# A two-block transformer kernel: the start in two channel halves, and four adaptive sums shared between VectorE, GpSimd and TensorE

## What is computed

```
c_act = silu(c)                                    # c: 1024 numbers
mod = c_act @ w_ada + b_ada                        # w_ada: 1024 x 6144
shift1, scale1, gate1, shift2, scale2, gate2 = split(mod, 6)
h = rms_norm(x, norm1_w) * (1 + scale1) + shift1
proj = h @ w_in                                    # gq, gk, gv, gz, ga, gb, sq, sk, sv
qkv = silu(causal_conv(concat(gq, gk, gv), conv_w, width 4))
...  gated delta rule on 8 heads, window attention on 8 heads
x = x + gate1 * (concat(o_g, o_s) @ w_out)
h2 = rms_norm(x, norm2_w) * (1 + scale2) + shift2
x = x + gate2 * ((silu(h2 @ w_gate) * (h2 @ w_up)) @ w_down)
```

## Time and profile before

| | |
|---|---|
| median of 3 runs | 1274.04 us (1273.92 to 1275.78) |
| profiled execution, its own time | 1273.12 us |
| its span in the profile | 1271.2 us |
| PE busy | 1221.3 us, 96% of the span |
| DVE, ACT, POOL busy | 701.7, 492.0, 107.0 us |
| chain that ended last | PE 91%, DVE 3%, DMA 2%, ACT 2% |

### The profile page before, as it was taken

How to read it: one execution, slowest core, us unless ns; L and a number is a source line. 1 busy time by engine, 2 the same in 40 slices (tenths; PEclk the granted TensorE clock), 3 DMA queues, 4 the chain that set the end, 5 groups by cost and what they waited for, 6 DMA issues and landing times.

```text
span 1271.2 us, 20461 instructions
## 1 busy us (share of the span) xinstructions
PE 1221.3 (96%) x8672; PEld 994.5 (78%) x8672; DVE 701.7 (55%) x1018; ACT 492.0 (39%) x774; POOL 107.0 (8%) x151
## 2 busy tenths in 40 slices
PE   2899999997999999999999999999999999999998
PEld 2577788787878888888888889798767678888886
DVE  4699878654468544323333457758456546334344
ACT  4543543665246323112222344223446663232232
POOL 4000004621011000000000110000012320000000
PEclk9899999999999999999999999999999999999999
DMA  9666621000222535233322343333231115433311
GB/s 311 219 209 184 219 66 36 3 3 31 74 67 71 163 105 160 81 111 104 100 87 63 86 146 94 100 92 76 41 79 46 34 47 134 115 87 87 114 40 67
DMA packets 150955, 125.62 MB, mean 99 GB/s; under 512 B 16985, under 2 KB 134514, under 8 KB 150737
## 3 DMA queue, kind: packets, MB, share of 16 engines
q1 hardware_dynamic: 147888, 119.88, 31.3%
q0 software_dynamic: 1232, 2.07, 0.5%
q10 hardware_dynamic: 1744, 2.36, 0.5%
HBM read 122.20 MB, written 2.10 MB: 98 GB/s over the span
## 4 chain that ended last, share of the span: by engine, by line
PE 91%; DVE 3%; DMA 2%; ACT 2%; issue 1%; POOL 0%; ACTq 0%; DVEq 0%; POOLq 0%
PE bank L583 56%; PE bank L676 5%; PE bank L825 5%; PE bank L1255 4%; PE bank L1226 4%; PE bank L1289 3%; PE bank L1143 2%; DMA arena<-in_meta_tokens_dram 1%; PE bank L988 1%; PE bank L1117 1%; PE bank L834 1%; PE bank L1176 1%; PE bank L1198 1%; PE bank L1156 1%; PE bank L797 1%
## 5 line engine op out<-in xcount | busy, mean ns | idle before, releaser
L583 PE MATMUL bank<-hsplit,whi 128*128 128x512 f32 (+1 forms) x1872 | 551.9, 379 | 0.7 <-DVE wlo L2005 0.7
L583 PEld LDWEIGHTS bank<-hsplit,whi 128*128 128x128 f32 x1872 | 341.2, 188 | 73.0 <-issue 8.0
L583 PE MATMUL bank<-hsplit,wlo 128*128 128x512 f32 (+1 forms) x936 | 352.3, 376 | 0.0
L2005 DVE TENSOR_TENSOR wlo<-ring,whi 128x2048 fp32r<-128x2048 f32 (+4 forms) x97 | 196.9, 2029 | 178.1 <-ACT whi L1485 177.8
L1485 ACT ACTIVATE whi<-ring 128x2048 fp32r<-128x2048 f32 (+4 forms) x97 | 165.4, 1705 | 129.3 <-DVE xT L2355 53.3
L583 PEld LDWEIGHTS bank<-hsplit,wlo 128*128 128x128 f32 x936 | 175.9, 188 | 33.1
L583 PE MATMUL bank<-a_split,whi 128*128 128x512 f32 x340 | 104.6, 389 | 0.0
L583 PEld LDWEIGHTS bank<-a_split,whi 128*128 128x128 f32 x340 | 63.8, 188 | 13.2
L583 PE MATMUL bank<-a_split,wlo 128*128 128x512 f32 x170 | 66.1, 389 | 0.0
L2034 DVE SCALAR_TENSOR_TENSOR post<-ring,small,post 128x512 f32<-128x512 f32 x77 | 57.9, 752 | 3.1 <-DMA ring<-in_w_ada_dram 0.4
L1426 POOL TENSOR_TENSOR acc<-acc,tb 128x512 f32<-128x512 f32 x12 | 17.7, 1478 | 426.2 <-ACT tb L1723 426.2
(11 more groups left out here) (443 smaller groups left out, 1726.2 us busy)
## 6 DMA issues: line engine op xcount, KB each, us to landing
ring<-in_w_ada_dram SPq DMA_DIRECT2D x24, 1024.0 KB, 5.2
ring<-in_w_in_dram SPq DMA_DIRECT2D x22, 1024.0 KB, 5.3
ring<-in_w_in_dram SPq DMA_DIRECT2D x34, 512.0 KB, 5.1
ring<-in_w_gate_dram SPq DMA_DIRECT2D x11, 1024.0 KB, 5.4
ring<-in_w_up_dram SPq DMA_DIRECT2D x11, 1024.0 KB, 5.2
ring<-in_w_down_dram SPq DMA_DIRECT2D x8, 768.0 KB, 4.9
ring<-in_w_down_dram SPq DMA_DIRECT2D x8, 640.0 KB, 4.5
ring<-in_w_out_dram SPq DMA_DIRECT2D x4, 1024.0 KB, 5.3
```

Source lines behind the costliest of these rows:

```text
L583: last = mm(o[0:m, 0:n], w[:, k, c0:c0 + m], rhs(s, k), start=k + i == 0, stop=k == kn - 1 and i == 2)
L2005: split_lo = splitter(dve, None, lambda lo, src, hi: tt(lo, src, hi, ALU.subtract))
```

## The change

- The ring loses `ada0` to `ada3`. They get places of their own, and SP issues x, `ada2`, `ada0`, `qkv0`, `ada3`, `ada1`, `qkv1`, `qkv2` without a wait. c comes as eight rows and is turned by PE.
- For i = 0 to 3 DVE sums only the first 512 rows. PE takes the second 512 straight from the panel: 16 matmuls of one column, and then the four of before.
- The modulation goes by channel halves: chunks 0 to 3 need columns i = 2 and 0, chunks 4 to 7 need i = 3 and 1. PE does `ada(3)` after chunk 1 and `ada(1)` after chunk 3 of the first tiles.
- DVE copies four chunks of x out of PSUM, ACT the other four.
- The meta tokens' columns come after the first tiles, their scaling after DVE's convolution of tile 1.
- For i = 4 to 7 DVE sums the first 512 rows; POOL makes four products and three additions for the second; PE adds both sums in PSUM, with eight matmuls in place of four. The slot of `ada{i}1` is free when POOL is done, and POOL starts panel i when PE has finished `ada(i - 1)`.
- POOL also clears `gates`, which DVE did before.

```
+        early_ada = {(i, h): hscratch[:, (2 * n + h) * PANEL:(2 * n + h + 1) * PANEL] for n, i in enumerate((2, 0)) for h in range(2)}
+        early_ada |= {half: C1.take(PANEL) for half in ((3, 0), (3, 1), (1, 0))}
...
+        POOL_ADA = range(4, 8)
+        pool_acc, pool_tmp = acc_buf[:, 0:512], row_buf
...
-        for i in range(4):
-            ada_panel(i)
...
+            def ada(i):
+                o = open_tile(pe, "ada", i)
+                if i < 4:
+                    pe.wait_ge(*ada_loaded(i, 1))
                     for k in range(4):
-                        last = mm(o[0:1, :], cs[:, 4 * h + k:4 * h + k + 1], W(f"ada{i}{h}")[:, k, :],
-                                  start=h + k == 0, stop=h == 1 and k == 3)
-                    last.then_inc(*(fill("adar", i) if h else signal("adarow_half", i)))
...
                 pe.wait_ge(*done("adaacc", i))
                 for c in range(4):
-                    last = mm(o[:, c:c + 1], adaacc[i % 2][:, c * P:(c + 1) * P], ones[:, 0:1], start=True, stop=True)
+                    last = mm(o[:, c:c + 1], acc_of(i)[:, c * P:(c + 1) * P], ones[:, 0:1], start=c == 0 if i in POOL_ADA else i >= 4,
+                              stop=i >= 8 or i < 4 and c == 3)
+                if i in POOL_ADA:
+                    pe.wait_ge(*done("poolacc", i))
+                    for c in range(4):
+                        last = mm(o[:, c:c + 1], pool_acc[:, c * P:(c + 1) * P], ones[:, 0:1], start=False, stop=c == 3)
...
+            tr(open_tile(pe, "c")[:, 0:KD], c_rows, ident[0:KD, 0:KD]).then_inc(*fill("c"))
+            pe.wait_ge(*arrived("x"))
...
-            ada(0)
+            pe.wait_ge(*copied("c"))
+            ada(2)
+            norm_spread("1", diag)
...
-            ada(1)
-            norm_spread("1", diag)
-            o = open_tile(pe, "spreadmeta")
-            pe.wait_ge(*done("dve_vectors", "diagmeta"))
-            mm(o[:, 0:META], ones[0:META, :], rbc[0:META, 0:META], start=True, stop=True).then_inc(*fill("spreadmeta"))
-            ada_rows(3)
-            ada(2)
-            ada_turn(3)
+            ada(0)
+            def meta_columns():
...
-                    first_tiles("qkv0", h_ready("1"), [(("pj", c), P * c, T, hx) for c in range(2)])
+                    first_tiles("qkv0", h_ready("1"), [(("pj", c), P * c, T, hx) for c in range(2)],
+                                between={1: [(ada, 3)], 3: [(ada, 1)]})
+                    meta_columns()
...
+            def load_ada(i):
+                for h in range(2):
+                    sp.dma_start(ada_half(i, h), w_cols(w_ada, 512 * i, 512, 4 * h, 4)).then_inc(sem(f"ld_ada{i}{h}"), 16)
+            sp.dma_start(x_in, a["x"][0].rearrange("(b p) f -> p b f", p=P)).then_inc(sem("ld_x"), 16)
+            load_ada(2)
+            load_ada(0)
             for i, (name, kn, width, parts) in enumerate(panels):
+                if name == "qkv1":
+                    load_ada(3)
+                    load_ada(1)
+                if name == "ada40":
+                    sp.dma_start(consts[:, CONST_FIRST:], a["consts"][:, CONST_FIRST:]).then_inc(sem("ld_const_rest"), 16)
...
+                    if before[:3] == "ada" and int(before[3:-1]) in POOL_ADA:
+                        sp.wait_ge(*done("poolacc" if before[-1] == "1" else "adaacc", int(before[3:-1])))
...
+            pool.wait_ge(*done("adaacc", 1))
+            nc.gpsimd.memset(gates, 0.0).then_inc(*signal("gates0"))
+            for i in POOL_ADA:
+                pool.wait_ge(*loaded(f"ada{i}1"))
+                if i > 4:
+                    pool.wait_ge(*filled("ada", i - 1))
+                w = W(f"ada{i}1")
+                for k in range(4):
+                    dst = pool_tmp[k % 2] if k else pool_acc
+                    nc.gpsimd.tensor_tensor(dst, w[:, k, :], cs[:, 4 + k:5 + k].broadcast_to([P, 512]), ALU.mult)\
+                        .then_inc(*signal("poolmul", i, k))
+                    if k:
+                        pool.wait_ge(*done("poolmul", i, k))
+                        nc.gpsimd.tensor_tensor(pool_acc, pool_acc, dst, ALU.add)\
+                            .then_inc(*(signal("poolacc", i) if k == 3 else signal("poolsum", i, k)))
+                        if k < 3:
+                            pool.wait_ge(*done("poolsum", i, k))
...
+            act.dma_start(c_rows, a["c"][0].rearrange("(k p) -> k p", p=P)).then_inc(sem("ld_c"), 16)
...
-            for k in range(KD):
+            for k in range(KD // 2, KD):
                 act.wait_ge(*filled("x", k))
                 A(xT[:, k, :], bank("x", k)[:, :], ACT.Copy).then_inc(*read("x", k))
...
+            def modulate_half(half):
+                act.wait_ge(*done("modA1", half))
+                act.wait_ge(*copied("ada", half))
+                first = 4 * half
+                for k in range(first, first + 5):
+                    if k < first + 4:
+                        act.wait_ge(*done("xn1", k))
+                        A(hpre[:, k, :], hpre[:, k, :], ACT.Identity, scale=modA1[:, k:k + 1],
+                          bias=modT[:, k:k + 1]).then_inc(*signal("mod1", k))
+                    if k > first:
+                        act.wait_ge(*done("mod1", k - 1))
+                        hi_part("h1", (k - 1,), h_of("1", 0, k - 1), hpre[:, k - 1, :])
...
+            modulate_half(0)
+            modulate_half(1)
...
+                halves = 1 if i < 8 else 2
...
+            for k in range(KD // 2):
+                dve.wait_ge(*filled("x", k))
+                v.tensor_copy(xT[:, k, :], bank("x", k)[:, :]).then_inc(*read("x", k))
+            dve.wait_ge(*copied("c"))
+            ada_sum(2)
+            spread("1", diag)
             ada_sum(0)
...
+            scale_half(0)
+            ada_mod(0)
+            split_lo()
+            h_rest("1", range(2))
+            ada_sum(3)
+            h_rest("1", range(2, 4))
             ada_sum(1)
...
+            scale_half(1)
+            ada_mod(1)
+            h_rest("1", range(4, 8))
...
+                if m == 1:
+                    meta_scaled()
```

More of the change, by code:

```diff
@@ L266, in program, with ada_half, ada_loaded @@
         gate_acc = C1b.take(2 * P)
+        early_ada[1, 1] = C1b.take(PANEL)
+        POOL_ADA = range(4, 8)
+        pool_acc, pool_tmp = acc_buf[:, 0:512], row_buf
+        def ada_half(i, h):
+            return early_ada[i, h].rearrange("p (k n) -> p k n", k=4) if i < 4 else W(f"ada{i}{h}")
+        def ada_loaded(i, h):
+            return arrived(f"ada{i}{h}") if i < 4 else loaded(f"ada{i}{h}")
         diag3 = arena[:, 10 * T:11 * T].rearrange("p (b t) -> p b t", b=4)
@@ L283, in program, with acc_of @@
         adaacc = [post[:, 0:512], post[:, 512:1024]]
+        def acc_of(i):
+            return adaacc[{2: 0, 0: 1, 3: 0}.get(i, i % 2)]
         G1, G2 = Cut(arena, base1), Cut(hscratch)
@@ L1464, in _ @@
                 act.wait_ge(*done("xss", b))
-            A(hpre[0:META, 0:2, :], meta_in[0:META, :].rearrange("p (k t) -> p k t", k=2), ACT.Square,
-              accum_out=msum[0:META, 0:1]).then_inc(*signal("act_vectors", "mss"))
             act.wait_ge(*done("dve_vectors", "eps"))
-            act.wait_ge(*done("act_vectors", "mss"))
             A(sroot, ssum, ACT.Sqrt, bias=epsc, scale=1.0 / D).then_inc(*signal("act_vectors", "root1"))
-            A(msum[0:META, 0:1], msum[0:META, 0:1], ACT.Sqrt, bias=epsc[0:META, :], scale=1.0 / D)\
-                .then_inc(*signal("act_vectors", "rootmeta"))
-            for k in range(KD):
+            for k in range(KD // 2, KD):
                 act.wait_ge(*filled("x", k))
                 A(xT[:, k, :], bank("x", k)[:, :], ACT.Copy).then_inc(*read("x", k))
-            act.wait_ge(*filled("meta"))
-            A(hmeta, bank("meta")[:, 0:8 * META], ACT.Copy).then_inc(*read("meta"))
             def root(tag, out, key, scale, bias):
@@ L1484, in _ @@
             A(V2[:, :], bank("vec")[:, P:P + V2_N], ACT.Copy).then_inc(*read("vec"))
+            act.wait_ge(*arrived("meta"))
+            A(tball[0:META, 0:D], meta_in[0:META, :], ACT.Square, accum_out=msum[0:META, 0:1]).then_inc(*signal("act_vectors", "mss"))
+            act.wait_ge(*done("act_vectors", "mss"))
+            A(msum[0:META, 0:1], msum[0:META, 0:1], ACT.Sqrt, bias=epsc[0:META, :], scale=1.0 / D)\
+                .then_inc(*signal("act_vectors", "rootmeta"))
             split_hi = splitter(act, lambda hi, src: A(hi, src, ACT.Copy), None)
@@ L1509, in _ @@
             split_hi()
-            act.wait_ge(*filled("adar", 3))
-            A(row_buf[1][0:1, :], bank("adar", 3)[0:1, :], ACT.Copy).then_inc(*read("adar", 3))
-            act.wait_ge(*done("dve_vectors", "modA1"))
-            modulate("1", modA1, 0)
+            modulate_half(0)
+            modulate_half(1)
             split_hi()
@@ L1535, in _ @@
                     conv_in(m)
+                    if m == 1:
+                        act.wait_ge(*filled("meta"))
```

(24 more changed lines are left out.)

93 lines of the change are left out of this document (36 added, 57 removed).

## The result

The change makes the kernel slower: 1289.72 us median of 6 runs (1287.69 to 1295.22) against 1274.01 for the kernel before, a ratio of 1.0129 [1.0108, 1.0149]. The profiled execution took 1288.9 us, with a span of 1287.0 against 1271.2: +15.8.

A forecast was written before the change was run, and what follows sets the result against it. PE, busy 96% of the span, was taken as the bound. Start -0.3, extra matmuls +3.9 and waits +5.9 gave +9.5 on 1273.12, so 1282.6, with the median 0.9 above: 1283.5 us, range 1274.5 to 1293.

The forecast's parts named there:

- Steps 1 to 4: Start: x loaded by 9.2 us, transposed by 14.3, `ada(2)` done at 20.3, `norm_spread` and the vectors at 22.7.
- step 3: Start, `ada(2)`: 20 matmuls mostly at the high clock, 15.1 to 20.3 us, with DVE's half sum about 3.1.
- Steps 5 to 8: From `ada(0)` (6.1 us) through first projection at 32.2, first tiles and meta columns: tile 2 at 62.1, start -0.3 us.
- My bound of +8: The start's upper bound: with the clock low throughout it gives +19 us, of which +8 was kept.
- Step 9: Tiles 2 to 11, PE: eight matmuls in place of four in `ada(4)` to `ada(7)`, 3.9 us, not hidden.
- Step 10: Tiles 2 to 11, DVE: saves 12.5 us of sums, worth nothing where PE never waited for them.
- Step 11: Tiles 2 to 11: POOL and DVE alternate, 11.7 us a panel on POOL; DVE loses 5.3 a panel, 21 in all.
- Step 12: After tile 4: a late panel split holds up ACT's squares, so PE waits 2.4 us.
- Step 13: `qkv5` queues behind `ada61`, whose slot waits for POOL: PE waits 2.3 us after tile 8, then 1.2 for `abk`.
- POOL and DVE don't hinder each other: Rival for the middle: start as forecast, then only PE's extra +3.9 us, 1277.6; chance 0.12.
- two rivals in which the start pays: Start -7.5 us: with no waits later 1270.4 (chance 0.10), or with the middle taking back 9.8, 1276.3 (0.12).
- low clock nearly throughout: Rival: `ada(2)` and `ada(0)` 8.6 us each, first projection near 39, tile 2 at 70, +8 + 9.8: 1292; chance 0.13.

The follow-up runs named there:

- `start_only`: The changed kernel's start with the middle of the kernel before, in which POOL sums nothing: 1278.93 us, ratio 1.0040 to the kernel before.
- `pool_narrow`: The changed kernel with POOL's products and additions over 32 of the 512 columns: 1281.85 us, ratio 1.0058 to the kernel before.
- `dve_pad`: `start_only` with seven more two-input DVE operations behind each of the sums for i = 4 to 7, and nothing on POOL: 1299.13 us.
- `pool_beside`: `start_only` with POOL also making 16 products and 12 additions from the constants, which no one uses or waits for in the tiles: 1299.48 us.
- `slot_free`: The changed kernel with POOL reading constants, and each second half's slot free once DVE has its half sum and the panel has landed: 1286.12 us.
- `middle_only`: The kernel before with POOL's part in the sums for i = 4 to 7 as in the changed kernel: 1287.65 us.

## Why the prediction was right, and where its sizes were off

The direction and the reason were right: 1283.5 was forecast, 1289.7 came, and a won start that PE pays back inside the first tiles, extra matmuls, and waits at `head_lengths` are all in the trace. The size was off: +15.7 for +9.5, inside the range but just outside the forecast's own band of 1278.5 to 1289. Most of the 6 us is a term of the clock, at the start and behind the wait. Point by point:

- **Steps 1 to 4** held: x at 10.1 (9.2), transposes to 15.98 (14.3), `ada(2)` to 20.4 (20.3), the vectors to 21.9 (22.7). DVE's half sum is 2.8 us by the earlier trace rows (0.5 and three of 0.78) and not the 3.1 of step 3; nothing waited for it.
- The page that the prediction weighed, the Trainium skill's "TensorE: Matmul & The Clock Gate", Part 4, by which transposes don't count as busy: the first `ada(2)`, straight behind the 32 transposes of x, ran at the high clock (3.70 us for 32 records, has 0.98 for 8), so this trace too speaks against it. In the nine profiles with this start those records took 3.70 to 4.84 us, and never the 6.84 of the low clock.
- **Steps 5 to 8**, the start at -0.3, were mis-sized: +4.3 in the profile and +5.9 by `start_only`. The term is the clock. `ada(0)` took 8.6 us and not 6.1, at 0.50 throughout, the first projection came at 33.6 and not 32.2, and chunks 2 and 3 took 4.8 and not 3.1, since `ada(3)` had let the clock fall. The two sums and the restart had nearly the right size (5.5, 5.8 and 3.1 for 5.2, 5.2 and 3.1). My bound of +8 held it.
- **Step 9**: 3.65 for 3.9, shown in the traces by blocks of 0.91 us and by `pool_narrow` (3.6 between the same two points); that fewer matmuls give it back the medians did not show.
- **Step 10** was wrong as a rule: "That is worth nothing where PE never waited for them." DVE had 0.5 us to spare in a round, and `dve_pad` shows 5.4 us more of its work costing 4.8 us a round. The half sum given away is worth much: `pool_beside`, where DVE keeps it, lost 19.1 us, and `slot_free`, where DVE gives it away and PE has the extra matmuls, 6.1.
- **Step 11**: a panel on POOL takes 12.2, 12.1, 11.7 and 10.9 us (11.7).
- **Step 12**: 1.3 us after tile 4 (2.4). `slot_free` still has this wait, so it is DVE's.
- **Step 13**: 4.3 us after tile 8 (2.3). POOL ended 0.4 later, its load was issued 0.4 after that, and the two panels took 1 us more to be split; and the term lacked the clock behind a wait of that length, 2.3 us. `slot_free` and `pool_narrow` show the wait gone with the hold. The wait for `abk` after tile 10 (1.2) did not come: by then, as I read it, the stand at tile 8 had given POOL that time. The waits came to 5.6 against 5.9 in all, but that is luck: one was too large, one too small, one absent, and the 2.3 of the clock stood in no term.
- **The rivals.** That POOL and DVE don't hinder each other is refuted by `pool_beside`; `pool_narrow` is the world in which they nearly don't, at 1281.85. The two rivals in which the start pays are refuted by tile 2 at 66.5 and by `start_only`. The low clock nearly throughout, at 1292, is nearer in number than the forecast (2.3 us off against 6.2) and half right in kind: `ada(0)` took the 8.6 that it gave, and tile 2 began at 66.5 to 70.1 in the nine profiles. But the first `ada(2)` ran high (3.70 us), and the first projection came at 33.6, not near 39.

## What to carry to other kernels

Ask for an engine's busy time in the stretch that the change touches, not in the span: DVE's 55% was 97% there, and everything added to it, by its own work or by a neighbour on its port, stood on the path. Work given to GpSimd is paid twice when its input lies in a ring slot: once on the shared port, and once in the queue behind that slot. Small matmuls go behind dense ones, early enough that the chain they feed runs beside the next dense piece; that order, together with 16 matmuls fewer on PE, turned this start from a loss of 5.9 us into a gain of 4.9.

## What the runs showed of the hardware

- A wait of 4.29 us in dense work was followed by 4.6 us at a granted clock of 0.50, so it cost half again as much; behind waits of 1.3 and 0.9 us the matmul took 1.02 and 1.05, behind waits of 2.2 to 2.5 us in six other kernels anything from 1.02 to 1.80. In `middle_only` the clock was also at 0.50 from 131 to 133 us, in dense work behind the one-column block for i = 6, with no wait ahead of it.
- POOL's price in time is the same as that of plain DVE work: +19.1 us with 28 POOL operations beside it, +19.1 with 28 more DVE operations. Even the DVE operation with one input rose from 0.48 to 1.26 us beside POOL (`pool_beside`, the first operation of the sum for i = 4).
- The same start ended anywhere within 3.6 us in nine profiles. The same 32 transposes of x took 5.78 to 6.66 us in them, and the two shortest stand in the two earliest starts; among the other seven the order is another, and the clock also rose and fell at other moments later on. The changed kernel's six runs spread over 7.5 us, the 49 of the kernel before over 4.0.
